# Rope rows turned by transfers within SBUF instead of a matmul, shared rope of the latent keys, Newton's step in two instructions

## What is computed

```python
def rmsnorm(x, g):
    y = xf * lax.rsqrt(jnp.mean(xf * xf, axis=-1, keepdims=True) + EPS)
    return (y * g.astype(jnp.float32)).astype(x.dtype)

def apply_partial_rope(x, cos, sin):
    half = ROPE_DIM // 2
    xr = x[..., :ROPE_DIM].astype(jnp.float32)
    x1, x2 = xr[..., :half], xr[..., half:]
    rot = jnp.concatenate([x1 * cos - x2 * sin, x2 * cos + x1 * sin], axis=-1)
    return jnp.concatenate([rot, x[..., ROPE_DIM:]], axis=-1)

# MLA: k_rope (B,S,MLA_ROPE) is shared over heads
k_pe = jnp.broadcast_to(k_rope[:, :, None, :], (b, s, MLA_HEADS, MLA_ROPE))
k = _rms_norm(jnp.concatenate([k_nope, k_pe], axis=-1), k_gain)
k = jnp.concatenate([k[..., :MLA_NOPE], _rope(k[..., MLA_NOPE:], positions)], axis=-1)
```

## Time and profile before

| | |
|---|---|
| time, median of 3 runs | 2482.09 us (2481.24 to 2483.05) |
| time of the profiled execution | 2479.0 us |
| its span | 2477.2 us |
| TensorE busy | 2429.3 us |
| VectorE, ScalarE, GpSimd busy | 1218.6, 928.7, 1316.0 us |
| mean granted clock | 0.994 |

### The profile page before, as it was taken

How to read it: one execution, slowest core, us unless ns; L and a number is a source line. 1 busy time by engine, 2 the same in 40 slices (tenths; PEclk the granted TensorE clock), 3 DMA queues, 4 the chain that set the end, 5 groups by cost and what they waited for, 6 DMA issues and landing times. The chain is left out here.

```text
span 2477.2 us, 29028 instructions
## 1 busy us (share of the span) xinstructions
PE 2429.3 (98%) x11174; PEld 1945.5 (79%) x11174; DVE 1218.6 (49%) x1937; ACT 928.7 (37%) x1447; POOL 1316.0 (53%) x1593
## 2 busy tenths in 40 slices
PE   7999999999999999999999999999999999999999
PEld 7767778888888888777687888888887667788887
DVE  4787756423224432359734843333323796266331
ACT  4444443322223223453524432332325454344321
POOL 4654346656556555446245665555553562456554
PEclk9999999999999999999999999999999999999999
DMA  5211123333333333212122333333332221323332
GB/s 174 76 60 60 52 69 94 95 102 94 96 100 106 100 96 100 68 61 68 43 78 84 94 94 102 94 95 100 95 100 60 68 60 43 94 85 95 94 100 96
DMA packets 59609, 213.37 MB, mean 86 GB/s; under 512 B 6608, under 2 KB 6736, under 8 KB 59344
## 3 DMA queue, kind: packets, MB, share of 16 engines
q1 hardware_dynamic: 59472, 211.52, 27.9%
HBM read 209.39 MB, written 2.10 MB: 85 GB/s over the span
## 5 line engine op out<-in xcount | busy, mean ns | idle before, releaser
L664 PE MATMUL banks<-t,t 128*128 128x512 f32 (+5 forms) x10854 | 2398.7, 390 | 26.9 <-POOL t L1839 17.3
L664 PEld LDWEIGHTS banks<-t,t 128*128 128x128 f32 (+1 forms) x10854 | 1908.7, 189 | 489.4 <-issue 84.2
L1839 POOL TENSOR_TENSOR t<-t,t 128x256 fp32r<-128x256 f32 x1548 | 1263.0, 848 | 1126.9 <-ACT t L1576 1126.9
L1576 ACT ACTIVATE t<-t 128x1024 fp32r<-128x1024 f32 x387 | 410.2, 1060 | 1172.6 <-issue 607.2
L1118 DVE TENSOR_TENSOR t<-banks,t 128x512 f32<-128x512 f32 x121 | 83.4, 689 | 201.1 <-PE banks L664 200.7
L1282 DVE TENSOR_TENSOR t<-banks,t 128x512 f32<-128x512 f32 x44 | 30.4, 691 | 183.6 <-PE banks L664 183.5
L1250 DVE SCALAR_TENSOR_TENSOR t<-banks,t 128x512 f32<-128x512 f32 x32 | 22.1, 692 | 155.4 <-PE banks L664 155.4
L1006 DVE SCALAR_TENSOR_TENSOR t<-t,t,t 128x512 fp32r<-128x512 f32 x64 | 51.5, 805 | 61.7 <-ACT t L1585 61.7
L1227 DVE TENSOR_TENSOR t<-t,t 128x512 fp32r<-128x512 f32 x68 | 70.1, 1031 | 2.3
L1256 DVE TENSOR_TENSOR t<-banks,t 128x512 f32<-128x512 f32 x24 | 16.6, 692 | 106.0 <-PE banks L664 106.0
L1277 DVE TENSOR_TENSOR t<-banks,t 128x512 f32<-128x512 f32 x44 | 30.4, 692 | 70.3 <-PE banks L664 69.9
(11 more groups left out here) (160 smaller groups left out, 1239.2 us busy)
## 6 DMA issues: line engine op xcount, KB each, us to landing
t<-in_w SPq DMA_DIRECT2D x387, 512.0 KB, 3.5
t<-in_xT SPq DMA_DIRECT2D x8, 256.0 KB, 5.9
out<-t SPq DMA_DIRECT2D x8, 256.0 KB, 4.6
t<-in_dmask SPq DMA_DIRECT2D x1, 1536.0 KB, 11.9
t<-in_vbias SPq DMA_DIRECT2D x2, 384.0 KB, 3.9
t<-in_c SPq DMA_DIRECT2D x1, 576.0 KB, 8.5
t<-in_pos SPq DMA_DIRECT2D x2, 256.0 KB, 6.2
t<-in_smask SPq DMA_DIRECT2D x1, 256.0 KB, 12.1
```

The source lines that it names most:

```text
L664: return pe.matmul(o, l, r, start=start, stop=stop, skip_group_check=True)
L1576: a.activation(whl[u % 2][:, 0:1024], wraw[u % 3][:, :], ACT.Copy).then_inc(*w_high.next(u))
L1839: p.tensor_tensor(hl[:, 1024:2048][:, c], wraw[u % 3][:, c], as_f32(hl[:, c]), ALU.subtract).then_inc(*w_low.next((u, q)))
```

## The change

- The turn matmul is gone. ScalarE now issues transfers from R to tile c, SBUF to SBUF, that swap the two halves of the rope rows: four of 8 rows for each of the 17 chains of the first block, two of 16 rows for each `mq` chain, 84 in all. They stand ahead of the square in ScalarE's list, and c is cleared once at the start so that other rows hold zero.
- `head_rope` waits for the transfers and multiplies c by a turned gain and the sine (now read from SBUF), then adds. The signs of the rotation go into the sine table.
- The Newton step is two instructions of three operands; a factor of -0.5/n goes into the gains once, at the start.
- The latent keys of a layer share one turned rope (`key_rope`, four instructions of 64 partitions on VectorE); each key's chain (`key_in`) has four ScalarE instructions of 64 partitions and no cosine, turn or transfer. The copies of L1397 are gone.
- Head chains have a queue of their own, first in, first out. The planner takes 0.05 us for the issue of such a transfer and 2.5 us until it has landed.

```diff
+TURN = {1: [(h + 8 - d, h + d, 8) for h in (0, 64) for d in (0, 8)], 2: [(80, 64, 16), (64, 80, 16)]}
+
+GAINS = [(n, 64) for n in ("qa", "ka", "qb", "kb")] + [(n, 96) for n in ("qg_0", "kg_0", "qg_1", "kg_1")]
+
+SHUFFLE = {1: [i ^ 8 if i < 16 else i for i in range(32)], 2: [i ^ 16 for i in range(32)]}
...
-            def head_turn(hid):
-                H = heads[hid]
-                bb = pair(H["slot"])[1]
-                reach(need, *H["src"], H["const"])
-                free(bb)
-                mm(B[bb], H["turn"], H["R"]).then_inc(*t_attn.next(("turn", hid)))
-                bank[bb] = [(v_attn, ("turned", hid))]
...
+                for k in (1, 2):
+                    v.tensor_reduce(SIGN[k], C[f"perm{k}"], AX, A_, negate=True).then_inc(*v_norm.next(("signs",)))
+                for n, width in GAINS:
+                    v.tensor_scalar(col(n), col(n), -0.5 / width, None, M_).then_inc(*v_norm.next())
+                need.wait_ge(*v_norm.last())
+                for n, width in GAINS[:4]:
+                    v.stream_shuffle(TURNED[n], col(n), SHUFFLE[1]).then_inc(*v_norm.next(("turns1",)))
...
+            def clear_turned():
+                for i, (a, b_, c) in enumerate(slot_tiles):
+                    v.memset(c, 0.0).then_inc(*v_norm.next(("clear",)))
...
             def head_rope(hid):
                 H = heads[hid]
                 a, b_, c = H["tiles"][H["slot"]]
-                need.wait_ge(*t_attn.at(("turn", hid)))
-                need.wait_ge(*t_attn.at(("sum", hid)))
-                v.tensor_tensor(a, B[pair(H["slot"])[1]], SIN, M_).then_inc(*v_attn.next(("turned", hid)))
+                reach(need, H["const"])
+                turned = in_turn[H["slot"]]
+                need.wait_ge(*turned.at(hid))
+                x = H["roped"]
+                v.scalar_tensor_tensor(out=c[x], in0=c[x], scalar=H["turned"][x], in1=SIN[x], op0=M_, op1=M_).then_inc(
+                    *v_attn.next())
                 need.wait_ge(*v_attn.last())
-                v.tensor_tensor(b_, b_, a, A_).then_inc(*v_attn.next(("roped", hid)))
+                v.tensor_tensor(b_[x], b_[x], c[x], A_).then_inc(*v_attn.next(("roped", hid)))
 
             def head_newton(hid):
                 H = heads[hid]
                 a, b_, c = H["tiles"][H["slot"]]
-                rsqrt(c, B[pair(H["slot"])[0]], H["n"], a, a_attn, ("head_rs", hid), v_attn, ("summed", hid),
-                      ("normed", hid))
+                need.wait_ge(*a_attn.at(("head_rs", hid)))
+                v.scalar_tensor_tensor(out=c, in0=B[pair(H["slot"])[0]], scalar=H["n"] * EPS, in1=c, op0=A_,
+                                       op1=M_).then_inc(*v_attn.next(("summed", hid)))
+                need.wait_ge(*v_attn.last())
+                v.scalar_tensor_tensor(out=a, in0=c, scalar=-3.0 * H["n"], in1=a, op0=A_, op1=M_).then_inc(
+                    *v_attn.next(("normed", hid)))
+
+            def key_rope(l):
+                need.wait_ge(*v_norm.at(("turns2",)))
+                need.wait_ge(*a_norm.at(("cos", 2)))
+                reach(need, branch[l]["small"], *branch[l]["lay"])
+                g, x = col(f"kg_{l}"), slice(64, 128)
+                v.stream_shuffle(KRS, KR, SHUFFLE[2]).then_inc(*v_attn.next(("key_turn", l)))
+                v.scalar_tensor_tensor(out=KRT, in0=KR, scalar=g[x], in1=COS[x], op0=M_, op1=M_).then_inc(*v_attn.next())
+                need.wait_ge(*v_attn.at(("key_turn", l)))
+                v.scalar_tensor_tensor(out=KRS, in0=KRS, scalar=TURNED[f"kg_{l}"][x], in1=SIN[x], op0=M_, op1=M_).then_inc(
+                    *v_attn.next())
+                need.wait_ge(*v_attn.last())
+                v.tensor_tensor(KRT, KRT, KRS, A_).then_inc(*v_attn.next(("key_rope", l)))
...
-                v.tensor_copy(MK[h][64:128, :], SM[64:128, :]).then_inc(*v_evac.next(("kr", l, h)))
...
+                a_, b_, c = H["tiles"][H["slot"]]
+                reach(need, *H["src"], *([H["before"]] if H["before"] else []), H["clear"])
+                for to, of, n in H["rows"]:
+                    a.dma_start(c[to:to + n], H["R"][of:of + n]).then_inc(*in_turn[H["slot"]].next(hid))
+                a.activation(a_, H["R"], ACT.Square).then_inc(*a_attn.next(("square", hid)))
+
+            def key_in(l, h):
+
+                hid = "mk", l, h
+                H = heads[hid]
+                a_, b_, c = H["tiles"][H["slot"]]
+                reach(need, *H["src"], branch[l]["small"], H["before"])
+                a.activation(a_[0:64, :], MK[h][0:64, :], ACT.Square).then_inc(*a_attn.next())
+                a.activation(a_[64:128, :], KR, ACT.Square).then_inc(*a_attn.next(("square", hid)))
+                a.activation(b_[0:64, :], MK[h][0:64, :], ACT.Copy, scale=col(f"kg_{l}")[0:64]).then_inc(*a_attn.next())
+                need.wait_ge(*v_attn.at(("key_rope", l)))
+                a.activation(b_[64:128, :], KRT, ACT.Copy).then_inc(*a_attn.next(("key_base", hid)))
...
-                rsqrt(c, B[pair(H["slot"])[0]], H["n"], a_, (v_attn, ("roped", hid)), a_attn, ("head_rs", hid))
+                rsqrt(a_, B[pair(H["slot"])[0]], H["n"], c, H["base"], a_attn, ("head_rs", hid))
...
-                need.wait_ge(*t_attn.at(("turn", hid)))
-                p.tensor_tensor(H["R"], b_, c, ALU.mult).then_inc(*p_attn.next(("head", hid)))
+                need.wait_ge(*H["base"][0].at(H["base"][1]))
+                p.tensor_tensor(H["R"], b_, a, ALU.mult).then_inc(*p_attn.next(("head", hid)))
...
-                yield "t", *k["src"], k["const"]
-                put("head_turn", hid)
                 yield "t", (a_attn, ("square", hid))
                 put("head_sum", hid)
-                yield "v", (t_attn, ("sum", hid))
+                yield "v", (in_turn[slot], hid)
                 put("head_rope", hid)
+                yield "a", (t_attn, ("sum", hid))
+                put("head_rs", hid)
+                yield "v", (a_attn, ("head_rs", hid))
+                put("head_newton", hid)
+                put("head_out", hid)
+                sch.done.add(hid)
+            return gen
+
+        def key_chain(l, h, **k):
+            hid = "mk", l, h
+            heads[hid] = k
+            k["base"] = a_attn, ("key_base", hid)
+
+            def gen(slot):
+                k["slot"] = slot
+                k["before"] = slot_head[slot]
+                slot_head[slot] = (p_attn, ("head", hid))
+                held[slot] = ((v_attn, ("summed", hid)),)
+                yield "a", *k["src"], (v_attn, ("key_rope", l))
+                put("key_in", l, h)
+                yield "t", (a_attn, ("square", hid))
+                put("head_sum", hid)
+                yield "a", (t_attn, ("sum", hid))
                 put("head_rs", hid)
                 yield "v", (a_attn, ("head_rs", hid))
                 put("head_newton", hid)
...
-            sch.waiting.insert(0, head_chain((n, t_), R=R, g=col(n), turn=PG[n], ones=C["bones"], n=64,
+            sch.heads.append(head_chain((n, t_), R=R, g=col(n), rows=TURN[1], roped=slice(0, 128), clear=(v_norm, ("clear",)), turned=TURNED[n], ones=C["bones"], n=64,
...
-        sch.until(("ka", 5), ("qa", 5))
+        sch.until(*[(n, t_) for n in ("qa", "ka") for t_ in (1, 3, 5)])
...
+            def key_item(slot):
+                yield "v", M["small"], (a_norm, ("cos", 2))
+                put("key_rope", l)
```

71 lines of the change are left out of this document (33 added, 38 removed).

## The result

The changed kernel takes 2470.4 us (median of six runs, 2467.5 to 2472.8) where the kernel before takes 2481.8 (six runs, 2477.7 to 2483.1): a ratio of 0.9955, with a 95% interval of 0.9942 to 0.9968. It is faster by 11.5 us, 0.45%. The forecast was 2456, 26 us faster: the direction holds, the size is less than half. 2470.4 lies outside the forecast's own 2448 to 2464 and inside the 2446 to 2476 that it gave for 8 in 10.

A forecast was written before the change was run, and what follows sets the result against it. The prediction took TensorE, busy 2429.3 of 2477.2 us, as the bound; -28.2 (turns) - 5 (keys) + 4 (circle) + 3 (MLA weight copies) = -26.2 us gave 2456 us, own range 2448 to 2464, 8 in 10 for 2446 to 2476.

The forecast's parts named there:

- Turn matmuls: All 33 head chains: one turn of 0.85 us each leaves TensorE, -28.2 us, with nothing else there to wait for.
- wrong at the root: Whole kernel: the prediction's own sign of failure, TensorE's idle time growing by over 15 us.
- Issue of 0.33 us: ScalarE's queue: each transfer issue takes 0.33 us, four 1.3 us, so TensorE's sum doesn't wait for the square.
- The circle: First block, issue to next issue through VectorE and ScalarE: 5.9 or 6.9 us against a 6.35 period; +4 us over 17 chains.
- The landing: Head chains' transfers: 2.1 us until a copy has landed, 3.5 as upper bound with a weight unit in the way.
- Newton and rope on VectorE: Each head chain: 4.86 us of VectorE work becomes 4.97, +0.1 a chain, off the bounding path while VectorE keeps up.
- Latent keys: MLA: 12 us less VectorE work a layer, TensorE's wait of 4.87 us a layer half gone; -5 us for two layers.
- Weight copies in MLA: MLA's eight query chains: weight copies that stand behind their squares cost 0.4 us each, +3 us.
- Start: Kernel start: at most 3 us of added VectorE work, hidden in a 14.7 us wait for ScalarE; nothing.
- The first, late transfers: First block: slower issues and landing put the circle 1.25 or 2.3 us over the period; 2473 or 2491 us; chance 0.20.
- The second: First block, 100 to 180 us: VectorE becomes the bound at 99% busy; total -15.7, 2466 us; chance 0.15.
- The third, all hidden: Circle stays under 6.35 us and MLA's waits go: -38 us, 2444 us; chance 0.10.

The follow-up runs named there:

- e1: Changed kernel in its own order, but the real program issues no transfers and waits for none (output lacks the turned part of the ropes); 2452.7 us.
- e6: Changed kernel with the turn as TensorE's matmul again in place of the transfers, all else as changed, planned anew; 2453.2 us.
- e2: Changed kernel in its own order, with the square ahead of the transfer issues in ScalarE's program; 2459.9 us.
- g4: The order of e5 with no transfer issued in the real program and no wait for one (output lacks the turned part of the ropes); 2443.2 us.
- e5: Changed kernel's real program in another order: planner told 0.33 us per issue and 2.0 to land, in place of 0.05 and 2.5; 2448.7 us.
- e7: Changed kernel with a VectorE shuffle in place of the transfers, in an order planned with the turn matmul, which real TensorE leaves out; 2453.7 us.
- f12: Changed kernel in its own order, with Newton's step in three VectorE instructions again; 2482.1 us.
- f11: Changed kernel with the latent keys' sharing undone: each key has its own rope chain with two transfers; 2495.1 us.
- e3: Changed kernel with the transfers issued from SyncE's queue in place of ScalarE's, at the same places of the order; 2520.2 us.
- e4: Changed kernel in its own order, with the rows turned by a stream_shuffle on VectorE in place of the transfers; 2455.9 us.

## Why the prediction was right in direction and wrong in size

The forecast was -26.2 us; what the profiled executions show, from the starts of the weight copies (unit 8 to 40 is the first block, 40 to 325 the MLA parts):

```
term                        on record   shown   from
33 turns                    -28.2       -28.2   taken as on record
transfers, first block       +4         +13.1   changed kernel against e1
transfers, MLA parts         +3          +7.1   changed kernel against e1
order, first block          none        +17.1   e1 against before, 14.5 of turns set aside
keys, Newton, order, MLA     -5         -16.2   e1 against before, 13.6 of turns set aside
sum                         -26.2        -7.1
```

**Turn matmuls, -28.2.** The 33 turns went. "Nothing lies beside it that TensorE would wait for instead" is the failed half: in the first block TensorE's idle grew by 20.1 us. Over the whole kernel it grew by 13.5 (47.9 to 61.4), just under the 15 us at which the prediction called itself wrong at the root, since MLA's waits shrank. e6 puts 25 of the turns back and is faster than the changed kernel.

**Issue of 0.33 us, "so the sum doesn't wait": the first step that failed.** It is 0.63, four in a row 2.62. The square comes 2.66 us after the first issue, and TensorE waits 0.9 us for it in the chain shown, 16.5 in all. The price was bounded by 0.44 from above, from copies of 128 rows; the bound was a guess about form. The Trainium skill ("DMA: Bandwidth & Descriptors", Why a DMA increments its semaphore by 16 and not by 1) gives 512 sequencer cycles for a copy instruction of previous generations, an estimate of 0.43 us; the trace is half as much again above it. What the prediction drew from it, that many small copies on a compute engine cost, was right: e1 measures 17.6 us for the 84. But the wait for the square isn't how they cost it in the first block (e2); there it is the next step.

**The circle, 5.9 or 6.9 us, +4.** It is 7.53. Four issues and the landing take 3.97 us until the product starts, where about 3 were expected, and the product waits 1.28 us, over the 1 that was named. The landing was right (2.0 us from the last issue's start to the product, 2.1 assumed). The addition was taken at its mean, 0.78, where the earlier trace rows have one of 1.65 in this very place. The next evacuation, which stands behind the addition in VectorE's list, isn't in the circle on record. The term was multiplied by 17, but additions stand 8.2, 7.6, 7.5 and 7.5 us apart over the first five chains only; from there on attention items set the rhythm. Its own size was 5 x 1.2 = 6 us at most; e1 shows 13.1 for the first block's transfers, and the rest of it wasn't followed chain by chain.

**What has no term: the order.** The sum took the list of before with pieces taken out. The planner wrote another. With no transfer at all (e1), units 8 to 40 still take 286.9 us where the kernel before takes 284.2, though 14.5 us of turns are gone: 17.1 us. At least 9.8 of these are the order, since g4 has the same instructions in e5's order and takes 277.1; whether the rest is order or an edit on VectorE and ScalarE wasn't told apart. The loss shows between units 36 and 38 (26.5 us), though not all of that is loss, since what stands at the end doesn't stand beside the dense groups (e7). e5 has the same real instructions as the changed kernel and is 21.7 us faster. Why the planner's order reacts so strongly to a price that changes by tenths wasn't settled: 0.05 with 2.5, 0.10, 0.33 and 0.66 with 2.0 leave 134, 54, 80 and 172, in no order.

**Newton and rope on VectorE, +0.1 a chain, hidden.** The mean durations of the five instructions sum to about 4.8 us (4.97 on record), so the size was about right; "hidden" was not: f12's 0.64 us more a chain cost 11.8 us. Had the two-operation product been reckoned against the two instructions in its place as its own edit, it would have shown as a gain.

**Latent keys, -5: under-sized.** Its own 3.6 us a key make 14.3 us a layer and not 12, but that slip is small beside the miss. MLA's wait went from 9.7 to 1.3 us, where half was on record, and without transfers the two MLA parts are 16.2 us shorter than before beside their turns, of which f12 puts 5.9 on Newton's step; the rest is the sharing together with whatever the new order does there. Without the sharing and with 16 more transfers (f11) they take what they took before, 1779.5 against 1780.5 us, though 16 turns are gone from them.

**Weight copies in MLA, +3.** e1 shows 7.1 for the 16 transfers there, and e2 gets the same 7 back by the place of the square alone. An estimate puts 3.6 of them on the clock (2 x 60 us x 0.03): in 1100 to 1160 and in 1940 to 2000 us it is 0.97 in the changed kernel and 1.00 in e2. The rest is open.

**Start, 0.** At unit 8 the traces stand 0.1 us apart. The other kernels of this order stand there 1.2 us earlier to 1.3 later, so no more than that is shown.

**Rivals.** The first, late transfers, was nearest: its 2473 us is 3 from the result. Its price per chain, 1.25 us over the period, is what the regular chains show (7.53 - 6.35 = 1.18), but through long issues and a slow addition and not through the landing, and on 5 chains, not 17. That its total fits is luck: the order's loss fills it up. The second isn't there: VectorE is busy 65.3 of 80 us in 100 to 180 us, 82%, not 99%. The third, all hidden at 2444, is what is reached with no transfer at all, in e5's order: 2443.2 (g4, which leaves the turning out).

```profile
100.00:180.00 80.00, 74.35 (x326) 53.32 (x326) 65.33 (x99) 37.89 (x69) 50.87 (x53) 1.00 0.27 74
```

## What to carry to other kernels

Where a planner writes the order, a change of one price rewrites places that the edit never touched: compare the traces by the start of each unit of work that both share, time the same instructions in two orders before an edit is praised or blamed, and try several prices, since a true one need not give the best list (here 2448.7 us with a wrong one, 2467.2 with the measured one). Price a small copy by a copy of its own form, and look at what stands behind it on its queue: the square here, a weight load's wait in e3. A wait that goes isn't yet time that comes back (e2). Follow each circle through the in-order lists of all engines, and take durations from the place in question, not from the group's mean.

## What the runs showed of the hardware

- A copy of 8 or 16 rows within SBUF takes 0.63 us to issue on ScalarE's queue and 0.62 on SyncE's (medians of 84), where a weight load of 128 rows takes 0.33 on SyncE's. An activation that stands ahead of the issues runs beside them (99.36 and 99.37 us above), one that stands behind waits for all four.
- VectorE's addition of two SBUF tiles, 128x512, took 0.69 us alone and 1.67 in the four places where it started 0.6 us behind GpSimd's multiplication L1892 and ran 1.12 us beside it; the multiplication took 1.75 us there and about 1.29 in most other places. One addition alone, beside the 1.67 of 104.59 above:

```profile
113.73 0.69 DVE L1147 TENSOR_TENSOR t<-t,t 128x512 f32<-128x512 f32 x1
```

  The Trainium skill ("SBUF — State Buffer", Who interferes with whom) says that a VectorE instruction with two SBUF inputs contends with a GpSimd instruction that reads SBUF, and that the port pair which they share is an exclusive lock; the trace agrees, to within the 1.0 us that the addition grew and the 1.12 it overlapped.
- A shuffle takes the same time for few rows as for many: in the kernel of e4, 128x512 and 32x512:

```profile
L1138 DVE STREAM_SHUFFLE t<-t 128x512 f32<-128x512 f32 x17 | 12.6, 740 | 0.0
...
L1138 DVE STREAM_SHUFFLE t<-t 32x512 f32<-32x512 f32 x8 | 5.8, 728 | 0.3
```
